# One more chunk of layer 1 by seven block products, paired adds of the second products' banks, and two new order tables

## The reference, cut to what matters

```
layer 0: y = (B * conv3(C * h)) W_out,  [B|C|h] = x W_in
layer 1: y = (trailing mean over 2/4/8/16 frames - x) W_grp * scale
h = layer_norm(ALPHA*x + y)
r = relu(h @ mlp_w1)                                 # 1024 -> 4096
f = (r*r) @ mlp_w2                                   # 4096 -> 1024
e = (p @ ple_w) * sigmoid(h @ ple_gate_w)
x = layer_norm(ALPHA*h + f + e)
```

## Time and profile before

| | us |
|---|---|
| median of three runs | 2075.65 |
| profiled execution | 2076.33 |
| its span, first to last instruction | 2074.5 |
| TensorE busy | 2060.5 (99%) |
| VectorE busy | 1457.0 (70%) |
| ScalarE busy | 963.6 (46%) |
| mean granted TensorE clock | 0.997 |

### The profile page before, as it was taken

The page is one execution under the profiler, slowest core; times in us unless marked ns, Lnnn a source line. Parts: engine busy times, 40 slices in busy tenths (PEclk is TensorE's granted clock), DMA queues, the critical chain, the costliest instruction groups (busy, mean ns, idle before and its releaser), DMA issues.

```text
span 2074.5 us, 32126 instructions
## 1 busy us (share of the span) xinstructions
PE 2060.5 (99%) x12926; PEld 2057.3 (99%) x12926; DVE 1457.0 (70%) x2106; ACT 963.6 (46%) x1493; POOL 24.4 (1%) x39
## 2 busy tenths in 40 slices
PE   9999999999999999999999999999999999999998
PEld 9999999999999999999999999999999999999998
DVE  5332348888777667687788798888776676756576
ACT  4222223555444434446476565645444444355454
POOL 0000000000000000000000000000000000000000
PEclk9999999999999999999999999999999999999999
DMA  4010122443112222234344344421122221343443
GB/s 178 31 61 30 71 92 82 134 145 132 62 60 73 72 82 82 66 117 141 112 142 150 112 160 141 146 93 56 57 82 82 82 82 59 133 161 113 135 142 123
DMA packets 62851, 211.15 MB, mean 102 GB/s; under 512 B 9088, under 2 KB 12288, under 8 KB 62720
## 3 DMA queue, kind: packets, MB, share of 16 engines
q1 hardware_dynamic: 59696, 208.61, 29.5%
q10 hardware_dynamic: 3024, 0.70, 0.2%
HBM read 204.82 MB, written 4.46 MB: 101 GB/s over the span
## 4 chain that ended last, share of the span: by engine, by line
PE 99%; DVE 0%; DMA 0%; ACT 0%; SPq 0%; issue 0%
PE ps L984 33%; PE ps L985 32%; PE ps L986 32%; DMA x_raw<-x_t 0%; PE ps L1044 0%; DVE acc L1611 0%; PE ps L1045 0%; DVE w_split L898 0%; PE ps L1013 0%; PE ps L1050 0%; PE ps L1019 0%; ACT w_split L1215 0%; SPq L923 0%; PE ps L1009 0%; PE ps L1082 0%
## 5 line engine op out<-in xcount | busy, mean ns | idle before, releaser
L984 PE MATMUL ps<-h_hi,w_split 128*128 128x352 f32 x1968 | 635.0, 323 | 0.7 <-DVE acc L1748 0.7
L985 PE MATMUL ps<-h_lo,w_split 128*128 128x352 f32 x1968 | 630.3, 320 | 0.0
L986 PE MATMUL ps<-h_hi,w_split 128*128 128x352 f32 x1968 | 630.0, 320 | 0.0
L984 PE MATMUL ps<-r_hi,w_split 128*128 128x352 f32 x1634 | 527.4, 323 | 4.4 <-DVE w_split L898 4.4
L985 PE MATMUL ps<-r_lo,w_split 128*128 128x352 f32 x1634 | 523.9, 321 | 0.0
L986 PE MATMUL ps<-r_hi,w_split 128*128 128x352 f32 x1634 | 523.6, 320 | 0.0
L898 DVE TENSOR_TENSOR w_split<-w_raw,w_split 128x1024 fp32r<-128x1024 f32 x327 | 390.6, 1220 | 41.7 <-ACT w_split L1215 41.0
L1792 DVE TENSOR_TENSOR acc<-acc,ps 128x352 f32<-128x352 f32 x665 | 327.0, 516 | 125.4 <-PE ps L986 122.8
L1215 ACT CAST w_split<-w_raw 128x1024 fp32r<-128x1024 f32 x327 | 329.9, 1045 | 165.5 <-PE ps L986 162.3
L984 PEld LDWEIGHTS ps<-h_hi,w_split 128*128 128x128 f32 x1968 | 369.0, 187 | 1.6 <-DVE w_split L898 1.0
L985 PEld LDWEIGHTS ps<-h_lo,w_split 128*128 128x128 f32 x1968 | 369.8, 188 | 0.0
(11 more groups left out here) (176 smaller groups left out, 1685.4 us busy)
## 6 DMA issues: line engine op xcount, KB each, us to landing
w_raw<-w_stream SPq DMA_DIRECT2D x375, 512.0 KB, 3.3
x_raw<-x_t SPq DMA_DIRECT2D x4, 704.0 KB, 8.1
y_t<-acc SPq DMA_DIRECT2D x4, 704.0 KB, 6.4
w_raw<-p_t SPq DMA_DIRECT2D x6, 352.0 KB, 3.4
y_t<-acc SPq DMA_DIRECT2D x7, 176.0 KB, 2.0
w_raw<-w_stream SPq DMA_DIRECT2D x3, 256.0 KB, 5.1
x_raw<-x_t SPq DMA_DIRECT2D x4, 176.0 KB, 4.0
x_raw<-x_t SPq DMA_DIRECT2D x2, 352.0 KB, 5.9
```

The lines of the kernel that those rows point to most:

```text
L984: pe.matmul(out, wh, mov_h, start=first, stop=False, **more)
L985: pe.matmul(out, wh, mov_l, start=False, stop=False, **more)
L986: return pe.matmul(out, wl, mov_h, start=False, stop=last, **more)
```

## The change

`CLASSIC` becomes (3, 4): chunk 4 of layer 1 is formed by the seven products too. Its four up steps of 24 matmuls become seven products of 12, and the sums of halves of layer 1 are asked for one chunk earlier, right behind downs B. The adds of a down step with two blocks become one VectorE instruction over both banks, [128, 2, 352], which waits for both and raises `b_free` by two. There are 320 such steps. Both tables are written anew; a line or two of each stands here.

```diff
-CLASSIC = (3,5)
+CLASSIC = (3,4)
 PLACES = [
-    (8, 8, 9, 9, 10, 10, 10, 10, 11, 12, 12, 13, 13, 14, 15, 15, 16, 17, 18, 18, 18, 19, 19, 20, 20, 20, 20),
+    (8, 8, 9, 9, 10, 10, 10, 10, 11, 11, 12, 12, 12, 14, 14, 14, 15, 16, 17, 17, 17, 18, 19, 19, 19, 19, 20),
...
 REFILLS = {
-    4: 1, 5: 4, 6: 3, 7: 3, 8: 2, 9: 3, 10: 2, 11: 4, 12: 7, 13: 6, 14: 3, 15: 4, 16: 4, 17: 5, 19: 1, 21: 1, 23: 1, 25: 1,
+    4: 1, 5: 2, 6: 3, 7: 3, 8: 3, 9: 2, 10: 2, 11: 1, 12: 4, 13: 5, 14: 4, 15: 4, 16: 3, 17: 6, 18: 1, 20: 1, 21: 1, 22: 2,
...
@@ in the walk of VectorE
+                elif step.kind == "down" and len(step.blocks) == 2:
+                    at, bank = step.n * GCOLS + step.blocks[0] * TG, B_BANK + step.bank
+                    pair = acc[:, at:at + 2 * TG].rearrange("p (k t) -> p k t", k=2)
+                    dve.wait_ge(b_full, step.b + 2)
+                    dve.tensor_tensor(pair, pair, ps[:, bank:bank + 2, 0:TG], ALU.add).then_inc(b_free, 2)
                 elif step.kind == "down":
                     for i, m in enumerate(step.blocks):
```

## The result

The changed kernel took 2084.6 us (median of five runs, 2082.2 to 2087.3) beside 2076.0 us for the kernel before (2074.6 to 2077.4): ratio 1.0041, 95% interval 1.0029 to 1.0052, so slower by 0.4%. The forecast was 2083.8 us, range 2080.0 to 2089.0. The profiled execution took 2084.6 us with a span of 2082.6 us, 8.1 us more than before (2074.5).

What follows compares the result with a forecast made beforehand. TensorE, busy 99% of the span, was taken as the bound: 2076.33 - 1.91 (matmuls) - 0.32 (mean) + 8.96 (VectorE's queue) + 1.4 (clock) = 2084.5 us profiled, 2083.8 us beside the median, range 2080.0 to 2089.0.

Steps and rivals of the forecast that it cites:

- Matmuls and mean: Layer 1's 12 removed matmuls, -1.91 us; the mean's two matmuls moved into the wait before the first gate tile, -0.32 us.
- The two waits of 2.2 us: TensorE's two waits for the second group tile's low part; neither table can shorten them, 0 us.
- Paired adds by themselves: Down steps with two blocks: a pair occupies VectorE 0.80 us instead of 0.87; no TensorE wait where VectorE keeps up, 0.
- product 6: One of layer 1's seven products, needing VectorE's third low part: starts at 1435.8 us instead of 1426.84, a 2.8 us wait.
- The queue of VectorE: Layer 1, about 1406 to 1436 us: VectorE's packed work delays TensorE as one debt, 8.96 us in all.
- B3: Third step of downs B in layer 1, reusing the first step's banks: waits 5.8 us for its paired add.
- B4: Fourth step of downs B in layer 1: could start at 1426.9 us, starts at 1427.3, a 0.4 us wait.
- The three near misses: Low parts for products 5, 7 and 3 in layer 1, predicted just in time: 1437.0 for 1437.7, 1438.6 for 1439.6, 1443.8 for 1445.3.
- The clock: TensorE's clock falling after the new gaps of layer 1: 1.4 us added, ends 0 and 2.8.
- VectorE keeps up: Rival: layer 1's VectorE work causes no wait and only the removed matmuls count; 2073.4 us, chance 0.06.
- the debt is partly paid: Rival: less queue work in layer 1 or the clock stays up, leaving 4 to 7 us; about 2079 us, chance 0.06.
- more waits: Rival: a second late place, or a near miss with a second clock fall, adds 3 to 7 us; 2087 to 2091, chance 0.11.

Runs made afterwards that it cites:

- e9: The kernel before, with 13 filling matmuls in each of its two 2.2 us waits and no other edit: 2074.7 us, ratio 0.9993.
- e7: The changed kernel with VectorE's layer 1 work spread, single adds, and 13 filling matmuls in each of the two 2.2 us waits: 2072.26 us, ratio 0.9982.
- e1: The changed kernel with the adds of a down step done one bank at a time, as before: 2082.69 us, ratio 1.0033.
- e2: The kernel before, with its own tables and chunks, and only the paired adds: 2078.67 us, ratio 1.0010.
- e3: The changed kernel, paired adds kept, with layer 1's half sums begun earlier, low parts moved and unneeded layer norm work later: 2075.29 us, ratio 0.9998.
- e6: The changed kernel with VectorE's layer 1 work spread and single adds in place of paired ones: 2073.31 us, ratio 0.9984.
- e10: The changed kernel with VectorE's layer 1 work spread, paired adds, and 13 filling matmuls in each of the two 2.2 us waits: 2072.67 us, ratio 0.9990.
- e4: The changed kernel with one more 128x1408 VectorE add (1.53 us) ahead of the first paired add of downs B: 2083.78 us, ratio 1.0033.
- e5: The changed kernel with TensorE kept busy by 34 and 16 unread matmuls in its two waits of layer 1: 2083.2 us, ratio 1.0032.
- e8: The changed kernel unaltered, run again for a second trace: 2083.18 us, ratio 1.0034.

## Why the prediction was right

**The bound.** Right. Time moved only with TensorE's matmuls, its waits and its clock.

**Matmuls and mean.** Right: 12 fewer. From the first gate tile's wait to the first 2.2 us gap both traces of the changed kernel take 637.19 us (1012.13 - 374.94 and 1012.01 - 374.82) where before took 637.62 (1012.40 - 374.78): -0.43 us, where -0.32 was predicted for the mean; 0.7 became 0.4 us of wait. e9 against e7 gives 2.4 us for both terms together, predicted 2.2.

**The two waits of 2.2 us.** Right, unchanged.

**Paired adds by themselves.** The size was right: 885 ns each, rows 0.79 to 0.80 us apart. The zero is a little low. It rested on the condition that VectorE keeps up. Where it doesn't, pairs cost something: 0.5 us at product 6 in the changed kernel (e1), and two waits of 0.39 and 0.33 us on the tables of before (e2). In the spread kernel no wait is for a pair. Yet with pairs the medians were higher each time they were compared (2.3 us in e2, 2.0 for e3 beside e6, 0.4 for e10 beside e7), in e3 and e10 by single long runs, and why stays open.

**The queue of VectorE.** Right, and it carries the result: 9.28 us measured, 8.96 predicted. B3's wait was 5.81 us for 5.8. e3 took the wait away and the loss went, e4 added 1.53 us and product 6 came 1.59 us later. How the debt showed behind B3 was not as predicted: I had B4 waiting 0.4 us and product 6 2.8 us. With the clock at half speed behind B3's gap, TensorE was itself later, B4 found its bank free, and product 6 waited 0.87 us. With the clock kept up (e5) B4 did wait, 0.23 us. The sum is nearly the same, since VectorE sets where product 6 starts; 0.24 of the 9.28 us are VectorE's own idle time ahead of B3's pair add. The three near misses behind it (T1, Y, the fourth half sum) were all in time.

**The clock.** The mechanism stood in the text with both ends, 0 and 2.8, and the value taken, 1.4, was not paid where I put it. The fall behind B3 was not quite free, as I had argued: e5, without it, has product 6 0.4 us earlier. Behind product 6's short gap (0.87 us, 1.36 us in the second trace) it didn't fall at all. Instead the fall that before had at 1012 us was absent from the first trace (-1.7 us) and present in the second.

**Not foreseen.** The slower spacing of matmuls, 2.6 us in the first trace, none in the second. It stands beside the missing fall in such a way that the profiled total of 2084.6 us meets the predicted 2084.5 us closer than the terms deserve. Part of the match is luck: the second trace, with before's clock falls and no slow spacing, came to 2082.9 us. The nine runs of the changed kernel have their median at 2083.4 us.

**The rivals.** "VectorE keeps up" and "the debt is partly paid" fell with the 5.8 us; "more waits" with the list of waits, which has no other that belongs to the change.

## What to carry to other kernels

Where one engine is 99% busy, an edit that saves work there is paid from the schedule of its helper: lay out the helper's queue by the spacing of its rows between two deadlines, and a fully packed stretch shows the loss before it is built. Spread such work over steps where the helper idles, and move what nobody wants yet behind it; here that turned 2084.6 us into 2075.3 us with paired adds and 2073.3 us with single ones, with the same matmuls. A short wait of TensorE that can't be removed is worth filling with matmuls that nobody reads, which made the runs alike to 1.4 us and, with the spread places, gave the best version of all, 2072.26 us (ratio 0.9982).

## What the runs showed of the hardware

- **The clock falls behind a short gap by chance.** Nine traces have the two gaps of 2.2 us (2.36 us once) unfilled. Behind 9 of these 18 gaps the granted clock fell to its lower level for a few us (111 to 114 matmuls in 22 us where 122 or 123 stand otherwise): in five traces behind the first alone, in two behind the second alone, in one behind both, in one behind none. A fall costs about 1.5 us, 10 matmuls or so at 0.1589 us each. Between the two gaps lie 165.74 to 165.96 us in the six traces with a fall behind the first (1177.84 - 1012.01 = 165.83 in e8) and 164.24 to 164.72 us in the three without (1176.37 - 1012.13 = 164.24 in the first trace). Behind the gaps of 5.1 to 7.3 us it fell in 4 traces of 4, behind those of 0.8 to 1.4 us in none of 4. The Trainium skill (TensorE: Matmul & The Clock Gate, the section on the HAM clock gate) says that the number of slow matmuls at a kernel's start differs from run to run; the traces show a chance in the middle of a kernel too. Its section on HAM oscillation has a fall behind every long wait, and the trace agrees for the four gaps of 5.1 us and more; the waits that it describes are longer than 2.2 us, so the chance behind the short gaps is what the runs add, and the prediction took that rule too far when it applied it to short gaps.
- **A slower spacing at full clock.** Matmuls that are 158.9 ns apart in every kernel stood 160.0 ns apart for some 370 us in one trace and 160.6 ns apart (75 us for 467) for about 90 us in another, with a granted clock of 1.00 and no gap. Both began behind a short wait, and both kernels have paired adds. Single runs 3 to 6 us above the others of the same kernel at nearly the same mean clock were seen with paired adds (the changed kernel, e3, e10) and in two of nine runs of e1, which has single adds and the 5 us wait; none in the 33 runs of e6, e7 and e9. What causes it stays open.
- **An add over two PSUM banks** costs as much as one of the same width in SBUF: 885 ns (128x704, one operand in PSUM) beside 887 ns.
